# Background projections by 512 columns and half of the tokens, in place of 256 columns and all tokens, in a two-layer encoder on one Trainium2 core

## The chip, the core and the metric

The kernel runs on one core of one Trainium2 chip. The metric is the device time of one execution in microseconds. The core's engines are TensorE (PE in the profile; PEld is its weight load), VectorE (DVE), ScalarE (ACT), GpSimd (POOL) and SyncE (SP, which here issues the weight loads). Each runs its own instructions in the order in which they are written and waits for the others by semaphores.

## What is computed

Two encoder layers over 768 tokens (a prompt of 512 and a sample of 256) with 1024 channels. One combined input projection feeds a gated linear attention branch (GLA) and a grouped-query attention branch; each is gated by a SiLU and projected, and the two are merged by sigmoid gates.

```python
def layer(x, norm_g, w_in, ...):
    h = rmsnorm(x, norm_g)
    proj = h @ w_in
    qa, ka, va, gfl, gbl, za, qb, kb, vb, zb, ma, mb = jnp.split(proj, split_points(), axis=-1)
    ya = gla_branch(qa, ka, va, gfl, gbl, za, w_gate_f, b_gate_f, w_gate_b, b_gate_b,
                    gla_norm_g, w_branch_a)
    yb = attn_branch(qb, kb, vb, zb, q_norm_g, k_norm_g, w_branch_b)
    merged = jax.nn.sigmoid(ma) * ya + jax.nn.sigmoid(mb) * yb
    return x + merged @ w_out
```

In `gla_branch` the output of the linear attention is normalised per head of 256 channels, multiplied by `silu(za)` (1024 gate columns) and projected. In `attn_branch` the queries and keys are normalised per head and get rotary positions before the attention.

## The kernel before

**Products in three passes.** Everything is float32. Each operand of a large product is split into a high part (fp32r) and the rest, so a product takes three matmul passes (high by high, high by low, low by high). For a weight block SP loads `w_raw`, ACT copies it to `w_hi` (`split` on ACT, L915), POOL subtracts to make `w_lo` (`split` on POOL, L1336). The weights lie in a ring of four slots (`RING`). The ACT split number i writes the slot of block i + 3 and waits (`w_used`) until TensorE has used block i - 1; SP loads the next block into a slot once its `w_lo` is made.

**Background.** Only part of the projection is made in a stage of its own. The other columns (`qb` to `mb`, and `za`) are made as *background*: TensorE puts their passes between the small, dependent products of the later stages. A background block is one of the 8 row blocks (`KT`) of the weights by 256 columns (`BGW`), used for all six tiles of 128 tokens (`NT`), which is 6 tiles x 3 passes of 256 columns. Eight blocks finish a group of 256 columns by 768 tokens, summed in three PSUM banks (5, 6, 7; in the rotary stage alternately 2, 3, 4). ACT then copies the three banks to the staging tile `stg` (L930, `copy_sums`) and stores it to a DRAM tensor `proj` (`store`). TensorE may write a bank again when `bg_free` says that ACT has copied it.

**Stages of a layer, and the order in them.** The order is written out by hand in each engine's program.

- GLA start: ACT and VectorE compute the gates of the first head while TensorE does 8 background blocks.
- GLA heads: four heads, each of ten levels (`gla_levels`); in each level TensorE does small products, VectorE collects and scales, ACT merges, and TensorE fills in 6 to 11 background tiles (`GLA_DONE`). At level 5 ACT computes the next head's gates (L995) and then stores a finished group. 16 blocks per head.
- Rotary stage: TensorE does only background here, 5 groups = 40 blocks: one group of `zb` and the four groups of `za`. VectorE does 18 rotary pieces (`rope`, L1709, L1713, L1715), whose second factor comes from POOL (`rope_swapped`, L1382, two buffers), the normalisation of the four GLA heads (`value_norms`, L1692) and, for each `za` group, the multiplication by the SiLU that ACT left in `stg` (`gate_columns`, L1700). `sil_ready` tells VectorE that `stg` is filled, `sil_used` tells ACT that it may be overwritten. POOL does splits and rotary pieces in one queue.
- Attention: four groups of 20 softmax steps each, with 16 background blocks per group; `ATT_TILES` says how many background tiles TensorE does in each step.
- Branch and output projections: 512-column products that the change leaves alone.

A stage ends with `phase_end`: ACT, VectorE and POOL wait for all; TensorE goes on with background of the next stage where that is allowed.

Of the kernel before, what the change touches and what calls it, by code (L numbers as in the profile page):

```python
# [33 lines left out]
F32 = mybir.dt.float32  # L34
# [41 lines left out]
J_Q, J_K, J_V, J_ZB, J_MA, J_MB, NBG = 0, 4, 5, 6, 10, 14, 18  # L76
BG_BLOCKS = 2 * KT
BG_TILES = BG_BLOCKS * NT

ROPE_GROUPS = 5  # L80
# [14 lines left out]
def start_steps(block, first, done, blocks):  # L95

    return {i: -1 if i * NT < first else next((n for n, d in enumerate(done) if i * NT < d), len(done))
            for i in range(block, block + blocks)}
# [3 lines left out]
GLA_FIRST, ATT_FIRST = KT * NT, 20  # L102
# [3 lines left out]
GLA_DONE = spread(GLA_FIRST, GLA_STEPS, (1, GLA_FIRST + 4), (5, GLA_FIRST + KT * NT), (9, GLA_TURN - 6), (GLA_STEPS, GLA_TURN))  # L106
GATE_STEP = 3
ATT_TAIL = 12
ATT_TILES = (3, 3, 3, 3, 2, 2, 3, 3, 4, 2, 3, 4, 4, 4, 3, 4, 4, 3, 4, 3)
ATT_DONE = [ATT_FIRST + sum(ATT_TILES[:n + 1]) for n in range(GROUP * UNITS)]  # L110
assert ATT_DONE[-1] == BG_TILES - ATT_TAIL and KT * NT in ATT_DONE
ATT_PIECE = 9
assert [ATT_DONE[ATT_PIECE + i] for i in (-1, 0)] == [KT * NT - 2, KT * NT]
PAIR_END = (1, 3, 4)
ATT_START = start_steps(0, ATT_FIRST, ATT_DONE, BG_BLOCKS)
GLA_START = start_steps(GLA_FIRST // NT, GLA_FIRST, GLA_DONE, BG_BLOCKS)
# [218 lines left out]
def trunk(nc, x_prompt, x_sample, norm_g, w_in, w_gate_f, b_gate_f, w_gate_b, b_gate_b, gla_norm_g,  # L335
# [37 lines left out]
    stg = sb("stg", [P, NT, BGW], R_G)  # L373
    proj = nc.dram_tensor("proj", [P, NBG, NT, BGW], F32, kind="Internal")
# [102 lines left out]
    with nc.Block() as block:  # L477

        @block.sync
        def _(sp):  # L480
# [26 lines left out]
            for layer in range(DEPTH):  # L507
# [5 lines left out]
                load_group(w_in, layer, C_QB, BGW)  # L513
                with at.repeat(GH, "gla background") as h:
                    for i in range(2):
                        load_group(w_in, layer, h * (2 * BGW) + C_QB + BGW + i * BGW, BGW)
                load_group(w_in, layer, C_ZB + 3 * BGW, BGW)
                with at.repeat(4, "rope background") as i:
                    load_group(w_in, layer, i * BGW + C_ZA, BGW)
                with at.repeat(KVH, "attention background") as g:  # L520
                    for i in range(2):
                        load_group(w_in, layer, g * (2 * BGW) + C_MA + i * BGW, BGW)
# [12 lines left out]
        def _(pe):  # L535
# [28 lines left out]
            def background(start, stop, bank0=BG_BANK, spare=0, ends=False):  # L564


                for u in range(start, stop):
                    i, t = divmod(u, NT)
                    k = i % KT
                    if t == 0:  # L570
# [4 lines left out]
                    out = ps[:, bank0 * HALF + t * BGW:bank0 * HALF + (t + 1) * BGW]  # L575
# [1337 lines left out]
```

## Time and profile before

| | us |
|---|---|
| median of 3 runs (2059.82 to 2060.16) | 2059.89 |
| the profiled execution's own time | 2061.01 |
| its span, first to last instruction | 2059.1 |
| TensorE matmul busy in the span | 1967.9 (96%) |
| VectorE, ACT, POOL busy | 987.4, 919.0, 736.1 |

The span is one execution as the hardware profiler saw it. The time that an execution reports is a little longer than the span. Matmuls are pipelined, so the busy time of single matmuls overlaps; the distance from start to start is what a pass costs. PEclk is the granted share of TensorE's full clock.

### The profile page before, as it was taken

What the parts mean: (1) busy time and instruction counts of PE and PEld (TensorE: products, weight loads), DVE (VectorE), ACT (ScalarE), POOL (GpSimd) and SP (SyncE); (2) the same over time, 40 slices, a digit from 0 to 9 for tenths busy, and PEclk for the clock granted to TensorE, in tenths of its full rate; (3) what the DMA queues carried; (4) which work ended last, traced back from release to release, by engine and by line L of the source; (5) the groups of instructions that cost most, each with busy time, mean ns of one, the idle gap of its engine ahead of it and who ended that gap; (6) DMA issues with size and microseconds to landing.
All of it is one profiled execution on the core that took longest, in us unless ns stands there. A gap on an engine that the chain in (4) does not pass through costs nothing.

```text
span 2059.1 us, 37278 instructions
## 1 busy us (share of the span) xinstructions
PE 1967.9 (96%) x13184; PEld 1817.1 (88%) x13184; DVE 987.4 (48%) x1397; ACT 919.0 (45%) x1816; POOL 736.1 (36%) x744
## 2 busy tenths in 40 slices
PE   5998999999999998999999989999999999989997
PEld 4988999999999997887799889999999999978786
DVE  4112555569755654324241045557686555633224
ACT  4213445533556665422441145545336656643233
POOL 3433222248432331333553332222682332323244
PEclk9999999999999999999999999999999999999999
DMA  4321222432121114331432121225221111152323
GB/s 146 93 59 42 73 60 66 139 102 65 37 65 46 56 46 145 111 117 62 126 98 77 51 57 62 66 69 158 81 58 47 46 61 53 54 175 71 118 87 138
DMA packets 122923, 168.92 MB, mean 82 GB/s; under 512 B 15696, under 2 KB 89296, under 8 KB 122832
## 3 DMA queue, kind: packets, MB, share of 16 engines
q1 hardware_dynamic: 82656, 107.52, 18.3%
q10 hardware_dynamic: 40176, 60.18, 8.5%
q8 instruction: 59, 0.97, 0.2%
q14 instruction: 32, 0.26, 0.0%
HBM read 136.19 MB, written 31.46 MB: 81 GB/s over the span
## 4 chain that ended last, share of the span: by engine, by line
PE 86%; DVE 5%; ACT 4%; issue 2%; ACTq 1%; DMA 1%; POOL 0%; DVEq 0%
PE ps L578 11%; PE ps L579 11%; PE ps L580 11%; PE ps L540 10%; PE ps L542 10%; PE ps L541 10%; PE ps L708 5%; PE ps L723 3%; PE ps L764 3%; PE ps L661 2%; PE ps L779 2%; PE ps L780 2%; PE ps L729 2%; PE ps L752 1%; PE ps L753 1%
## 5 line engine op out<-in xcount | busy, mean ns | idle before, releaser
L1336 POOL TENSOR_TENSOR w_lo<-w_raw,w_hi 128x256 fp32r<-128x256 f32 (+1 forms) x560 | 586.8, 1055 | 1254.6 <-ACT w_hi L915 1252.8
L578 PE MATMUL ps<-w_hi,act_hi 128*128 128x256 f32 x2112 | 611.6, 290 | 13.8 <-POOL w_lo L1336 8.6
L580 PE MATMUL ps<-w_hi,act_lo 128*128 128x256 f32 x2112 | 598.5, 283 | 0.0
L579 PE MATMUL ps<-w_lo,act_hi 128*128 128x256 f32 x2112 | 598.4, 283 | 0.0
L915 ACT ACTIVATE w_hi<-w_raw 128x256 fp32r<-128x256 f32 (+1 forms) x560 | 275.7, 501 | 515.1 <-PE ps L542 300.7
L578 PEld LDWEIGHTS ps<-w_hi,act_hi 128*128 128x128 f32 x2112 | 405.0, 192 | 19.9 <-POOL w_lo L1336 9.4
L579 PEld LDWEIGHTS ps<-w_lo,act_hi 128*128 128x128 f32 x2112 | 405.4, 192 | 2.7
L580 PEld LDWEIGHTS ps<-w_hi,act_lo 128*128 128x128 f32 x2112 | 405.2, 192 | 0.0
L540 PE MATMUL ps<-w_hi,o_hi 128*128 128x512 f32 x384 | 157.6, 410 | 9.3 <-DVE o_lo L1507 6.9
L542 PE MATMUL ps<-w_hi,o_lo 128*128 128x512 f32 x384 | 152.1, 396 | 0.0
L541 PE MATMUL ps<-w_lo,o_hi 128*128 128x512 f32 x384 | 151.7, 395 | 0.0
L1739 DVE TENSOR_REDUCE st<-ps 128x1 f32<-128x512 f32 (+1 forms) x160 | 109.4, 688 | 85.9 <-PE ps L753 85.9
L1094 ACT ACTIVATE pr<-ps,st 128x512 f32<-128x512 f32 (+1 forms) x192 | 117.2, 612 | 49.9 <-DVE st L1739 47.6
L1025 ACT ACTIVATE scaled<-scaled 128x768 f32<-128x768 f32 x64 | 53.3, 833 | 162.6 <-DVE scaled L1599 161.7
L1745 DVE TENSOR_TENSOR pt_lo<-ps,pt_hi 128x512 fp32r<-128x512 f32 x128 | 88.0, 688 | 45.2 <-ACT pt_hi L1104 42.9
L1104 ACT ACTIVATE pt_hi<-ps 128x512 fp32r<-128x512 f32 x128 | 76.6, 599 | 67.0 <-PE ps L780 52.4
L1615 DVE COPY_PREDICATED amat<-mask,ps 128x768 f32<-128x768 uint8 x56 | 58.0, 1036 | 99.0 <-issue 79.2
L708 PE MATMUL ps<-scaled 128*128 128x128 f32 x768 | 102.3, 283 | 0.0
L764 PE MATMUL ps<-ident,pr 128*128 128x128 f32 x640 | 96.3, 273 | 3.6 <-ACTq L1096 3.6
L540 PEld LDWEIGHTS ps<-w_hi,o_hi 128*128 128x128 f32 x384 | 73.5, 191 | 28.9 <-DVE o_lo L1507 7.5
L708 PEld LDWEIGHTS ps<-scaled 128*128 128x128 f32 x768 | 96.9, 192 | 0.3
L542 PEld LDWEIGHTS ps<-w_hi,o_lo 128*128 128x128 f32 x384 | 73.2, 191 | 16.1
(174 smaller groups left out, 3574.2 us busy)
## 6 DMA issues: line engine op xcount, KB each, us to landing
w_raw<-in_w_in SPq DMA_DIRECT2D x352, 128.0 KB, 2.1
proj<-stg ACTq DMA_DIRECT2D x36, 768.0 KB, 3.5
w_raw<-in_w_in SPq DMA_DIRECT2D x80, 256.0 KB, 2.7
w_raw<-in_w_out SPq DMA_DIRECT2D x64, 256.0 KB, 2.7
w_raw<-in_w_branch_a SPq DMA_DIRECT2D x32, 256.0 KB, 2.7
w_raw<-in_w_branch_b SPq DMA_DIRECT2D x32, 256.0 KB, 2.7
q<-proj ACTq DMA_DIRECT2D x8, 768.0 KB, 4.9
zb<-proj ACTq DMA_DIRECT2D x8, 768.0 KB, 9.7
```

Of the source, the lines that this page charges most:

```text
L540: mm(out, s_hi, m_hi, start=first, stop=False)
L541: mm(out, s_hi, m_lo, start=False, stop=False)
L542: return mm(out, s_lo, m_hi, start=False, stop=last)
L578: mm(out, act_hi[:, k, tok], w_hi[:, k % RING, 0:BGW], start=(k == 0 and t % 2 == 0), stop=False, skip_group_check=True)
L579: mm(out, act_hi[:, k, tok], w_lo[:, k % RING, 0:BGW], start=False, stop=False, skip_group_check=True)
L580: last = mm(out, act_lo[:, k, tok], w_hi[:, k % RING, 0:BGW], start=False, stop=(k == KT - 1), skip_group_check=True)
L708: last = mm(ps[:, j * P:(j + 1) * P], lhs, rhs, start=True, stop=True)
L764: last = nc.tensor.transpose(bank(pt_bank(n))[:, place * P:(place + 1) * P], pr[:, n % 2, j * P:(j + 1) * P], ident[:])
L915: A(w_hi[:, slot, 0:width], w_raw[:, slot, 0:width], ACT.Copy).then_inc(s.w_hi_done, 1)
L1094: last = A(pr[:, n % 2, i * w:(i + 1) * w], ps[:, n % 2 * HALF + i * w:n % 2 * HALF + (i + 1) * w], ACT.Exp, bias=nmax(n, i), accum_out=de ...
L1336: G.tensor_tensor(w_lo[:, slot, 0:width], w_raw[:, slot, 0:width], w_hi[:, slot, 0:width].bitcast(F32), ALU.subtract).then_inc(s.w_lo_done, 1)
L1739: V.tensor_reduce(out, view_ps(n % 2 * HALF, (HALF // k, k), (1, HALF // k)), AX.X, ALU.max, negate=True).then_inc(s.neg_max, 1)
```

## The change

A background block becomes 512 columns wide and serves three token tiles (`NH`), half of the tokens: 3 tiles x 3 passes of 512 columns. A pair of such groups (`pair`, half 0 and half 1) makes 512 columns for all tokens, so each weight block is loaded and split twice, once per half, in the GLA and attention stages. The number of blocks there stays (8, 16 per head, 16 per attention group); the tables of tiles per step are about halved. A tile fills a PSUM bank of its own.

In the rotary stage the 40 blocks become 24: the 1024 `za` columns are made as two groups of 512 columns for **all six** token tiles (`gate_columns` on TensorE, banks 5, 6, 7, 0, 1, 2 and then 3, 4, 5, 6, 7, 0), 8 blocks each of 6 tiles x 3 passes of 512 columns; then one half group of 8 blocks in banks 1, 2, 3. ACT still stages three tiles at a time in `stg`, so a six-tile group is handed to VectorE in two halves. VectorE's multiplications (now `gate_values`) and the `value_norms` stand at other rotary pieces, and the last one comes before the stage's end. POOL's rotary pieces are spread by `rope_block`. In the attention group the reciprocal of the sums (`sums_inverse(0)`) stands one step earlier.

```diff
+GATE_BANKS = (5, 6, 7, 0, 1, 2), (3, 4, 5, 6, 7, 0), 1
+ROPE_BLOCKS = 3 * KT
+def rope_block(n):
+    at = n * 5 * KT // (3 * NT)
+    return at // 2 if at < 4 * KT else at - 2 * KT
...
-ATT_TILES = (3, 3, 3, 3, 2, 2, 3, 3, 4, 2, 3, 4, 4, 4, 3, 4, 4, 3, 4, 3)
+ATT_TILES = (2, 1, 1, 2, 1, 1, 2, 1, 2, 1, 1, 2, 2, 2, 2, 1, 2, 2, 2, 2)
...
-    stg = sb("stg", [P, NT, BGW], R_G)
+    stg = sb("stg", [P, NH, HALF], R_G)
...
-                    if k == 0 and t % 2 == 0:
-                        pe.wait_ge(s.bg_free, at.peek("bg_free", 1 - 3 * spare))
+                    if k == 0:
+                        pe.wait_ge(s.bg_free, at.peek("bg_free", NH + 1 - back))
                         at.skip("bg_free", 1)
-                    mm(out, act_hi[:, k, tok], w_hi[:, k % RING, 0:BGW], ...)
-                    mm(out, act_hi[:, k, tok], w_lo[:, k % RING, 0:BGW], ...)
-                    last = mm(out, act_lo[:, k, tok], w_hi[:, k % RING, 0:BGW], ...)
+                    t = i // KT % 2 * NH + n
+                    last = three_passes(bank(bank0 + n), act_hi[:, k, t * P:(t + 1) * P], act_lo[:, k, t * P:(t + 1) * P],
+                                        w_hi[:, k % RING, :], w_lo[:, k % RING, :], k == 0, k == KT - 1)
...
+            def gate_columns(banks, behind):
+                def tile(k, t):
+                    if k == 0:
+                        if t == behind:
+                            pe.wait_ge(s.o_read, at.peek("o_read", 2))
+                            pe.sem_inc(s.passed, 1)
+                        pe.wait_ge(s.bg_free, at.peek("bg_free", NH + 1 - (NH if behind and t < NH else 8)))
+                        at.skip("bg_free", 1)
...
+                gate_columns(GATE_BANKS[0], NT - 1)
+                gate_columns(GATE_BANKS[1], None)
+                background(BG_HALF, 2 * BG_HALF, GATE_BANKS[2], 8)
...
-                for i in range(ROPE_GROUPS * KT):
-                    split(i % KT, BGW)
+                for i in range(ROPE_BLOCKS):
+                    split(i % KT)
                     if i == 0:
                         rsqrt_seed(NT * GH)
+                    if i in (KT - 1, KT, 2 * KT - 1, 2 * KT):
+                        pair, half = divmod(i - KT + 1, KT)
+                        if i == KT - 1:
+                            all_stored()
+                        else:
+                            act.wait_ge(s.sil_used, at("sil_used"))
+                        for n in range(NH):
...
+                            A(stg[:, n, :], bank(GATE_BANKS[pair][half * NH + n]), ACT.Silu).then_inc(s.bg_free, 1)
+                        act.wait_ge(s.bg_free, at("bg_free", NH))
+                        act.sem_inc(s.sil_ready, 1)
+                act.wait_ge(s.sil_used, at("sil_used"))
+                store(P_GATE, 1, GATE_BANKS[2])
...
-                    if n in (3, 7, 11):
-                        value_norms(n // 4)
-                    if n in (6, 10, 14):
-                        gate_columns(n // 4 - 1)
-                value_norms(3)
+                    if n in (2, 4, 10, 12):
+                        value_norms((2, 4, 10, 12).index(n))
+                    if n in (7, 8):
+                        gate_values(n - 7)
+                    if n == 14:
+                        gate_values(2)
+                        gate_values(3)
```

**VectorE in the rotary stage.** This is VectorE's queue before, from the norm behind rotary piece 3 to the first multiplication by a SiLU (`rot` are the rotary buffers, `va` the GLA values, `stg` ACT's staging tile).

```order
L1692 SCALAR_TENSOR_TENSOR va<-va,st,gv_row 128x256 x5
L1709 TENSOR_TENSOR rot_103<-q,cs 128x512
L1713 TENSOR_TENSOR rot_103<-rot_103,rot_104 128x512 [waits rot2_ready,dve_chain]
L1715 TENSOR_TENSOR q<-rot_103,st_qk 128x512 [waits dve_chain]
L1709 TENSOR_TENSOR rot_103<-kv,cs 128x256 [waits rot2_free]
L1713 TENSOR_TENSOR rot_103<-rot_103,rot_104 128x256 [waits rot2_ready,dve_chain]
L1715 TENSOR_TENSOR kv<-rot_103,st_qk 128x256 [waits dve_chain]
L1709 TENSOR_TENSOR rot_103<-q,cs 128x512 [waits rot2_free]
L1713 TENSOR_TENSOR rot_103<-rot_103,rot_104 128x512 [waits rot2_ready,dve_chain]
L1715 TENSOR_TENSOR q<-rot_103,st_qk 128x512 [waits dve_chain]
L1700 TENSOR_TENSOR va<-va,stg 128x6x256 [waits va_normed,sil_ready,rot2_free]
```

And now, from the second of the two norms that stand before it (piece 4) to the second multiplication.

```order
L1725 SCALAR_TENSOR_TENSOR va<-va,st,gv_row 128x256 x5
L1744 TENSOR_TENSOR rot_103<-kv,cs 128x256
L1748 TENSOR_TENSOR rot_103<-rot_103,rot_104 128x256 [waits rot2_ready,dve_chain]
L1750 TENSOR_TENSOR kv<-rot_103,st_qk 128x256 [waits dve_chain]
...
L1750 TENSOR_TENSOR q<-rot_103,st_qk 128x512 [waits dve_chain]
L1735 TENSOR_TENSOR va<-va,stg 128x3x512 [waits va_normed,sil_ready,rot2_free]
L1744 TENSOR_TENSOR rot_103<-kv,cs 128x256
L1748 TENSOR_TENSOR rot_103<-rot_103,rot_104 128x256 [waits rot2_ready,dve_chain]
L1750 TENSOR_TENSOR kv<-rot_103,st_qk 128x256 [waits dve_chain]
L1735 TENSOR_TENSOR va<-va,stg 128x3x512 [waits sil_ready,rot2_free]
```

The first multiplication has moved from behind piece 6 and one norm to behind piece 7 and two norms.

**ACT in the rotary stage.** Before, where a SiLU group ends: splits, the three copies of the finished group, and the next splits (`w_hi` are the split weights).

```order
L915 ACTIVATE w_hi<-w_raw 128x256 [waits w_used,w_slot2]
L930 ACT_TABLE_LOAD [waits stored]
L930 ACTIVATE stg<-ps 128x512 [waits w_used]
L930 ACTIVATE stg<-ps 128x512 x2
L915 ACTIVATE w_hi<-w_raw 128x256 [waits bg_free,w_used,w_slot3]
L915 ACTIVATE w_hi<-w_raw 128x256 [waits w_used,w_slot0]
```

And now.

```order
L944 ACTIVATE w_hi<-w_raw 128x512 [waits w_used,w_slot2]
L1260 ACT_TABLE_LOAD [waits bg_done]
L1260 ACTIVATE stg<-ps 128x512 [waits stored]
L1260 ACTIVATE stg<-ps 128x512 [waits bg_done] x2
L944 ACTIVATE w_hi<-w_raw 128x512 [waits bg_free,w_used,w_slot3]
L1260 ACTIVATE stg<-ps 128x512 [waits bg_done,sil_used]
L1260 ACTIVATE stg<-ps 128x512 [waits bg_done]
L1260 ACTIVATE stg<-ps 128x512 [waits w_used]
L944 ACTIVATE w_hi<-w_raw 128x512 [waits bg_free,w_used,w_slot0]
L944 ACTIVATE w_hi<-w_raw 128x512 [waits w_used,w_slot1]
```

Three copies stand at a group's end and one split later three more, which wait for `sil_used`, with all later splits behind them.

**POOL in the rotary stage.** Before, two or three `w_lo` of 256 columns stand between two rotary pieces (`rot_104` is POOL's factor).

```order
L1336 TENSOR_TENSOR w_lo<-w_raw,w_hi 128x256 [waits w_hi_done] x3
L1382 TENSOR_TENSOR rot_104<-q,cs 128x16x16 [waits rot2_free]
L1382 TENSOR_TENSOR rot_104<-q,cs 128x16x16
L1336 TENSOR_TENSOR w_lo<-w_raw,w_hi 128x256 [waits w_hi_done] x2
L1382 TENSOR_TENSOR rot_104<-q,cs 128x16x16 [waits rot2_free]
```

Now, from the end of piece 8 over the two splits behind it to piece 9 and one more split.

```order
L1415 TENSOR_TENSOR rot_104<-kv,cs 128x8x16
L1369 TENSOR_TENSOR w_lo<-w_raw,w_hi 128x512 [waits w_hi_done] x2
L1415 TENSOR_TENSOR rot_104<-q,cs 128x16x16 [waits rot2_free]
L1415 TENSOR_TENSOR rot_104<-q,cs 128x16x16
L1369 TENSOR_TENSOR w_lo<-w_raw,w_hi 128x512 [waits w_hi_done]
```

Each piece of POOL stands behind the split of its block, so behind TensorE's progress by blocks of twice the length.

## Rows read from the trace of the kernel before

**Rows 1.** The page's chain that ended last, shares of the span by engine.

```profile
PE 86%; DVE 5%; ACT 4%; issue 2%; ACTq 1%; DMA 1%; POOL 0%; DVEq 0%
```

**Rows 2.** Busy time in the stages of layer 0, from GLA start to attention.

```profile
core 0: us, PE busy (x) PEld busy (x) DVE busy (x) ACT busy (x) POOL busy (x), PEclk, DMA share, GB/s
178.30:202.70 24.40, 20.09 (x149) 19.60 (x150) 6.63 (x6) 14.69 (x17) 7.67 (x8) 0.93 0.15 39
202.70:438.50 235.80, 233.91 (x1789) 227.56 (x1788) 133.28 (x167) 114.75 (x197) 56.18 (x73) 1.00 0.29 89
438.50:527.00 88.50, 87.76 (x729) 87.59 (x730) 75.11 (x87) 29.56 (x71) 70.53 (x76) 1.00 0.26 71
527.00:810.00 283.00, 275.17 (x2177) 263.11 (x2175) 164.37 (x278) 176.14 (x418) 88.21 (x104) 1.00 0.17 53
```

**Rows 3.** Timeline, TensorE, passes of 256 columns: start, length in us.

```profile
600.00 0.28 PE L578 MATMUL ps<-w_hi,act_hi 128*128 128x256 f32 x1
...
600.36 0.28 PE L578 MATMUL ps<-w_hi,act_hi 128*128 128x256 f32 x1
```

**Rows 4.** Timeline, TensorE, passes of 512 columns.

```profile
149.79 0.39 PE L542 MATMUL ps<-w_hi,act_lo 128*128 128x512 f32 x1
...
150.47 0.39 PE L542 MATMUL ps<-w_hi,act_lo 128*128 128x512 f32 x1
```

**Rows 5.** Groups of POOL by shape: busy us, mean ns of one.

```profile
L1336 POOL TENSOR_TENSOR w_lo<-w_raw,w_hi 128x512 fp32r<-128x512 f32 x232 | 315.5, 1365 | 551.2 <-ACT w_hi L915 551.1
L1336 POOL TENSOR_TENSOR w_lo<-w_raw,w_hi 128x256 fp32r<-128x256 f32 x328 | 271.3, 836 | 703.4 <-ACT w_hi L915 701.7 <-issue 1.0
```

**Rows 6.** Groups of ACT by shape.

```profile
L915 ACT ACTIVATE w_hi<-w_raw 128x512 fp32r<-128x512 f32 x232 | 144.6, 629 | 357.6 <-PE ps L542 300.7 <-PEq L561 29.4 <-PEq L631 8.0
L915 ACT ACTIVATE w_hi<-w_raw 128x256 fp32r<-128x256 f32 x328 | 131.1, 411 | 157.5 <-PE ps L580 140.2 <-ACT stg L930 8.4 <-issue 4.3
```

**Rows 7.** Timeline, TensorE: rotary start, first key transpose behind the stage.

```profile
438.55 0.36 PE L578 MATMUL ps<-w_hi,act_hi 128*128 128x256 f32 x1 [0.29 <-issue]
...
530.27 0.82 PE L729 MATMUL ps<-ident,k_st 128*128 128x128 f32 x6
```

**Rows 8.** Timeline, VectorE, rotary stage; piece 7 ends before 480.04.

```profile
442.78 0.68 DVE L1709 TENSOR_TENSOR rot<-q,cs 128x512 f32<-128x512 f32 x1
...
460.18 4.97 DVE L1692 SCALAR_TENSOR_TENSOR va<-va,st,gv_row 128x256 f32<-128x256 f32 x6
...
475.08 1.76 DVE L1700 TENSOR_TENSOR va<-va,stg 128x1536 f32<-128x1536 f32 x1 [1.55 <-ACTq L1230]
...
480.04 4.48 DVE L1692 SCALAR_TENSOR_TENSOR va<-va,st,gv_row 128x256 f32<-128x256 f32 x6
```

**Rows 9.** Timeline, VectorE, end of the rotary stage.

```profile
524.67 2.46 DVE L1692 SCALAR_TENSOR_TENSOR va<-va,st,gv_row 128x256 f32<-128x256 f32 x6
527.55 1.76 DVE L1700 TENSOR_TENSOR va<-va,stg 128x1536 f32<-128x1536 f32 x1 [0.41 <-ACTq L462]
```

**Rows 10.** Timeline, ACT, first key copy of the attention.

```profile
529.00 0.85 ACT L1137 ACTIVATE k_st<-kv 128x768 fp32r x1
```

**Rows 11.** Groups of POOL in the rotary stage, by shape.

```profile
L1382 POOL TENSOR_TENSOR rot<-q,cs 128x256 f32<-128x256 f32 x24 | 24.4, 1038 | 0.0
```

**Rows 12.** Timeline, POOL, GLA start.

```profile
192.43 4.17 POOL L1336 TENSOR_TENSOR w_lo<-w_raw,w_hi 128x256 fp32r<-128x256 f32 x4 [3.85 <-ACT w_hi L915]
```

**Rows 13.** Timeline, TensorE, GLA start: the idle time before it.

```profile
194.59 0.48 PE L578 MATMUL ps<-w_hi,act_hi 128*128 128x256 f32 x1 [3.53 <-POOL w_lo L1336]
```

**Rows 14.** Timeline, ACT, level 5 of a GLA head.

```profile
285.73 1.67 ACT L995 ACTIVATE gate<-ps,bg_fix 128x768 f32<-128x768 f32 x2
...
287.60 1.57 ACT L930 ACTIVATE stg<-ps 128x512 f32<-128x512 f32 x3
```

**Rows 15.** Timeline, TensorE, level 5 of the last GLA head.

```profile
406.39 0.36 PE L578 MATMUL ps<-w_hi,act_hi 128*128 128x256 f32 x1 [1.57 <-ACT stg L930]
```

**Rows 16.** Waits of TensorE in the attention: us in total, times, longest.

```profile
PE ps L779 <- DVE q L1764: 1.7, 4, 0.4
```

More of the change, by code:

```diff
@@ L95, in start_steps @@
 def start_steps(block, first, done, blocks):
-    return {i: -1 if i * NT < first else next((n for n, d in enumerate(done) if i * NT < d), len(done))
+    return {i: -1 if i * NH < first else next((n for n, d in enumerate(done) if i * NH < d), len(done))
             for i in range(block, block + blocks)}
-GLA_FIRST, ATT_FIRST = KT * NT, 20
+GLA_FIRST, ATT_FIRST = BG_HALF, 10
 GLA_STEPS = len(LEVELS) + 1
@@ L574, in background @@
                         at.skip("bg_free", 1)
-                    out = ps[:, bank0 * HALF + t * BGW:bank0 * HALF + (t + 1) * BGW]
-                    tok = slice(t * P, (t + 1) * P)
-                    mm(out, act_hi[:, k, tok], w_hi[:, k % RING, 0:BGW], start=(k == 0 and t % 2 == 0), stop=False, skip_group_check=True)
-                    mm(out, act_hi[:, k, tok], w_lo[:, k % RING, 0:BGW], start=False, stop=False, skip_group_check=True)
-                    last = mm(out, act_lo[:, k, tok], w_hi[:, k % RING, 0:BGW], start=False, stop=(k == KT - 1), skip_group_check=True)
@@ L584, in background @@
                         last.then_inc(s.bg_done, 1)
+            def gate_columns(banks, behind):
[6 more added lines that the diff above has]
+                        at.skip("bg_free", 1)
+                    last = three_passes(bank(banks[t]), act_hi[:, k, t * P:(t + 1) * P], act_lo[:, k, t * P:(t + 1) * P],
+                                        w_hi[:, k % RING, :], w_lo[:, k % RING, :], k == 0, k == KT - 1)
+                    if k == KT - 1 and t < NT - 1:
+                        last.then_inc(s.bg_done, 1)
+                    return last
+                for k in range(KT):
+                    pe.wait_ge(s.w_lo_done, at("w_lo_done"))
+                    late = behind is not None and k < 2
+                    for t in range(NT - late):
+                        last = tile(k, t)
+                    if not late:
+                        last.then_inc(s.w_used, 1)
+                    elif k == 1:
+                        for early in range(2):
+                            tile(early, NT - 1).then_inc(s.w_used, 1)
@@ L787, in turn_out @@
                     at.skip("o_drained", 1)
[L789 removed]
+                background(0, 6)
                 for part in range(2):
@@ L1422, in attention_group @@
                         h += 1
-                    split(i, BGW if i + SKEW < BG_BLOCKS else HALF)
+                    split(i)
                 assert h == GROUP
@@ L1441, in _ @@
                 phase_ends()
-                for i in range(GLA_FIRST // NT):
-                    split(i, BGW)
+                for i in range(KT):
+                    split(i)
                 with at.repeat(GH - 1, "gla head") as h:
```

123 lines of the change are left out of this document (55 added, 68 removed).

## The prediction

> **What bounds the kernel now.** The chain of work that ended last comes first: 86% of it is TensorE [rows 1]. The stages then say how closely TensorE is packed: in the GLA heads it is busy for 233.9 of 235.8 us, in the rotary stage for 87.8 of 88.5, in the attention for 275.2 of 283.0 [rows 2]. So in those stages a shorter TensorE program shortens the kernel as long as nobody becomes later than it. In the rotary stage the reader should also see VectorE at 75.1 and POOL at 70.5 of 88.5 us [rows 2]: the next bound is near. The second layer repeats the first; I work out one layer and double it.
>
> **What the change gives TensorE.** Full-clock passes of 256 columns follow each other at 120 ns (three in 0.36 us, [rows 3]), passes of 512 columns at 227 ns (three in 0.68, [rows 4]). Two of the old are 240 ns, one new is 227: 13.3 ns less. A layer has 9 + 5 + 8 = 22 groups of 8 blocks x 18 passes = 3168 old passes, 1584 new ones: 1584 x 13.3 = 21.1 us, 42.2 for both layers. By stage: GLA start 1.0, GLA heads 7.7, rotary 4.8, attention 7.7. The price is in splits. A 512-column w_lo takes POOL 1.37 us and w_hi takes ACT 0.63, against 0.84 and 0.41 for 256 [rows 5, 6]. Over a block of 9 x 227 ns = 2.04 us this fits. The weight loads double in bytes; they run blocks ahead and I price them at nothing, since no load stands among TensorE's waits.
>
> The Trainium skill, page "TensorE: Matmul & The Clock Gate", section "Back-to-back issue gap", speaks against the change: start to start is columns / 2.4 GHz plus 2.5 ns. By it a merged pair saves only 2.5 ns, an estimated 8 us for both layers. The trace does not agree: over the streaming it shows 13 ns at both widths.
>
> **GLA start: +0.6.** TensorE waits 3.53 us for a w_lo here and then runs at half clock (granted clock 0.93 over 24.4 us, so 3.4 us at half, a loss of 1.7) [rows 2, 13]. ACT's gate functions stand ahead of the split. Each split on this path gets 0.22 longer on ACT and some 0.5 on POOL, or more: four w_lo of 256 took 4.17 there [rows 12], against 0.84 mean. I take +0.9 for the late w_lo, less 0.3 for the three blocks behind it: +0.6. The block behind it hides the rest. The wait was 3.5 and becomes 3.8, so the clock's loss stays.
>
> POOL's share of that wait bears on a rule of the Trainium skill, page "SBUF — State Buffer", section "Who interferes with whom": a VectorE operation with two SBUF inputs and a GpSimd one exclude each other for a whole instruction. By it a w_lo of 512 can hold VectorE for 1.3 us where one of 256 held it for 0.7, but half as often; the sum stays.
>
> **GLA heads: -4.3.** All 64 blocks save 7.7. At level 5 the gain is lost. ACT does gate magnitudes (285.73, 1.67 us), one split and then the first copy of the finished group, started at 287.60 and done 0.6 later [rows 14]; TensorE may not start the next group before. The background tiles ahead of this point shrink from 11 x 0.36 = 3.96 to 5 x 0.68 = 3.4, the ACT path grows by 0.2: per head 0.55 + 0.3 = 0.85 is waited instead of gained. In the last head, which already waits 1.57 there [rows 15], 0.6. Together 3 x 0.85 + 0.6 = 3.2, rounded with 0.2 for steps that now have 3.4 us of cover in place of 3.6 to 4.0: 7.7 - 3.4 = 4.3.
>
> **Attention: -7.5.** 4 x 16 blocks save 7.7. Where a group starts, the key transposes and the first scores wait for VectorE, not for background: there 0.2 a group is lost, 0.8 in all. Steps cut from 3 tiles (1.08 us) to 1 (0.68) stay above the chain, since TensorE waits little here, and one of its waits, 0.4 us a group before the value products [rows 16], is eased by the reciprocal that now stands a step earlier: 4 x 0.4 = 1.6 gained at most; I take 0.6, between that and nothing. So -7.7 + 0.8 - 0.6 = -7.5.
>
> **Rotary stage: +8.2, the term that decides.** TensorE starts at 438.55 [rows 7]. A six-tile block is 18 x 227 ns = 4.09 us. Group 0 ends at 471.3. Group 1 uses banks 3, 4, 5, 6, 7, 0; its last tile of its first block needs bank 0, which tile 3 of group 0 filled. TensorE gets there at 438.55 + 8 x 4.09 + 5 x 0.68 = 474.7. But ACT copies tile 3 only after `sil_used`, behind VectorE's first multiplication, and that now stands behind pieces 0 to 7 **and two norms**. In the trace VectorE ended piece 7 at 480.0, with one norm and the old multiplication (1.76 plus 1.55 waiting) done [rows 8]. Take these 3.3 out, put the second norm in (4.48) and the multiplication behind (1.76): 480.0 - 3.3 + 4.5 + 1.8 = 483.0, less 0.6 since POOL is a little less crowded: 482.4. A copy (0.6) later TensorE goes on: 483.1, after 8.4 us of waiting and with 1.7 lost to half clock as at the GLA start. Blocks 8 and 9 end at 483.1 + 4.77 + 1.7 = 489.6.
>
> The hold travels. POOL's piece 9 stands behind the split that needs block 9 used: 489.6 + 0.63 (ACT) + 1.3 (POOL) + 2 x 0.8 (piece; 1.04 each when crowded, [rows 11]) = 493.1, and VectorE, which wants it near 486.5, waits 6 us. From there its work up to the third multiplication is 5 pieces of about 2.8, two norms of 4.4, one multiplication of 1.8 and 2 us of waits: 493.1 + 26.6 = about 519.5. ACT stands before that with split 17 and all later ones behind it: three copies (1.6) and the split, w_lo at 522. POOL then has 7 splits of 1.3 and three pieces (1.7, 1.7, 1.3) = 13.8: stage end near 535.7. Before, it was when VectorE's last norm ended, 527.13 [rows 9], and the first key transpose on TensorE came 3.1 later, at 530.27 [rows 7, 10]. Now it comes at 538.8: 8.5 later; the 0.3 of background that is not hidden any more is given back. I take +8.2. TensorE's own gain of 4.8 is inside this number. Bounds from rows: below, the stage can't end before VectorE's work is done. That starts at 442.8 [rows 8]; 75.1 us of it [rows 2], 1.8 for the multiplication that moved in, 2.0 for the handover between the third and the fourth, 3 for the wait at the first piece: 524.7, or -2.4. Above, each later split on POOL as long as when crowded (1.4 to 2.1 a piece of w_lo) and a second half-clock stretch: +13.
>
> **Sum.** 0.6 - 4.3 + 8.2 - 7.5 = -3.0 a layer, -6.0 for both. The profiled execution took 2061.0, so 2055.0 for it; the median of the runs is 1.1 lower: **2054**.
>
> **Rivals.** A change of 0.2%, 4.1 us, is what a measurement of this kernel can tell.
> - *The rotary hold is light.* If VectorE speeds up whenever POOL stands idle (its norms took 2.46 in place of 4.97 with POOL quiet, [rows 8, 9]), the multiplication comes earlier, the cascade through piece 9 shrinks, and the stage ends within 0 to +6. Time 2038 to 2050. For it: those two rows. Against: before piece 7 POOL has eight pieces and nine splits to do. Chance 0.2.
> - *The rotary hold is heavier, and the kernel slower.* The third multiplication's hold stops split 17 and everything behind it. If VectorE comes there later than 519.5, each us moves the stage end one for one, and TensorE's second idle stretch halves its clock again (1.7). From +10.3 a layer the time is unchanged, from +13.2 it is slower by 0.2%. Time 2059 to 2068. For it: VectorE is the fullest engine after TensorE, and has 6 us of waits that I estimate. Chance 0.2.
> - *A wide pass costs more in the background than alone.* 227 ns is from a stage of nothing else. At 232 the 1152 passes of GLA heads and attention a layer cost 5.8 more: 2054 + 11.5 = 2065. Against: the 256-column pass is 120 ns amid the attention's small products [rows 3]. By the skill's rule for the gap the gain outside the rotary stage would fall by 10.8 x 1152 = 12.4 us a layer, an estimate of 2079. Chance 0.08, the skill's rule within it 0.02.
>
> **How the numbers follow.** Forecast (rotary +6 to +10.3): 0.52, range 2050 to 2058. Faster: the light hold (0.2) and most of the forecast (to +9.2, 0.40) = 0.6. Same: the rest of the forecast (0.12) and half of the heavy hold (0.12) = 0.24. Slower: 0.08 + 0.08 = 0.16. The range leaves out the far ends of the light and the heavy hold: 2042 to 2065.
>
> **What the profile after would show.** Passes at 227 ns. In the rotary stage a wait of TensorE of some 8 us, ended by ACT's copy, near 475; a wait of VectorE for POOL near 487; ACT waiting for VectorE's third multiplication; first key transpose near 538. In the GLA heads a wait of about 1 us a head for the copy at level 5. Attention group 68.4 us in place of 70.3. The prediction is wrong if TensorE runs through the rotary stage (then it is far too high), or if the steps of the attention, cut to one tile, now end in waits for ACT (then too low).

## The result: slower by 1.4%, and the profile after

| | before | after |
|---|---|---|
| median, us | 2060.02 (2059.82 to 2060.34, 4 runs) | 2088.96 (2088.49 to 2090.86, 4 runs) |
| ratio | | 1.0142, 95% interval 1.0124 to 1.0160 |
| span of the profiled execution | 2059.1 | 2086.7 |
| TensorE busy, mean granted clock | 1967.9, 0.992 | 1955.1, 0.984 |
| POOL, VectorE busy | 736.1, 987.4 | 859.6, 1020.1 |

TensorE's program did get shorter and the kernel got longer: 28.9 us slower where 6 us faster was forecast. The stages say where. A stage is measured from its first TensorE instruction to that of the next one (GLA start: first gate product; heads: first level product; rotary: first background pass behind the last head; attention: first key transpose; its end: first product of the branch).

| stage, us a layer | before, layers 0, 1 | after, layers 0, 1 | change forecast | change measured |
|---|---|---|---|---|
| GLA start | 24.4, 24.4 | 25.2, 25.2 | +0.6 | +0.8 |
| GLA heads | 235.9, 235.9 | 238.4, 238.4 | -4.3 | +2.5 |
| rotary | 91.7, 91.7 | 104.1, 104.2 | +8.2 | +12.4 |
| attention | 287.5, 287.3 | 286.6, 286.7 | -7.5 | -0.8 |
| sum | | | -3.0 | +14.9 |

Twice the last sum is 29.8; the untouched stages give some 2 back, which makes the 27.6 of the spans.

Busy time by stage of layer 0 of the changed kernel, with the columns of [rows 2] (windows chosen from its own stage starts; the third ends with VectorE's last rotary piece):

```profile
core 0: us, PE busy (x) PEld busy (x) DVE busy (x) ACT busy (x) POOL busy (x), PEclk, DMA share, GB/s
176.90:202.10 25.20, 20.84 (x77) 16.12 (x78) 7.22 (x6) 16.40 (x17) 11.38 (x8) 0.86 0.27 73
202.10:440.40 238.30, 230.86 (x1213) 197.68 (x1211) 144.67 (x167) 127.41 (x197) 92.60 (x74) 0.99 0.41 123
440.40:541.90 101.50, 87.53 (x373) 70.75 (x374) 79.88 (x88) 28.24 (x55) 66.72 (x60) 0.97 0.23 63
544.50:831.10 286.60, 273.45 (x1606) 227.56 (x1606) 167.21 (x282) 185.73 (x421) 113.24 (x103) 0.99 0.29 87
```

Read the heads first, against the second stage of [rows 2]. VectorE has the same 167 instructions and is busy for 144.7 us in place of 133.3: its own work did not change, each piece of it takes longer. The engine that did change is POOL, 92.6 in place of 56.2. The groups of POOL in the heads, before and then after:

```profile
L1336 POOL TENSOR_TENSOR w_lo<-w_raw,w_hi 128x256 fp32r<-128x256 f32 x64 | 48.8, 776 | 168.2 <-ACT w_hi L915 167.4 <-issue 0.5
```

```profile
L1369 POOL TENSOR_TENSOR w_lo<-w_raw,w_hi 128x512 fp32r<-128x512 f32 x65 | 86.3, 1345 | 134.8 <-ACT w_hi L944 134.3 <-issue 0.5
```

As many blocks, each twice as wide (the 65th lies at the window's edge): a weight block is now split once for each half of the tokens. The 37.5 us more on POOL are the price that the prediction set against TensorE's block time alone. The timeline shows them landing on VectorE. Level products of the second head, changed kernel; VectorE, POOL, TensorE, in this order:

```profile
272.81 2.04 DVE L1634 TENSOR_TENSOR scaled<-scaled,totals 128x768 f32<-128x768 f32 x1
```

```profile
270.76 3.27 POOL L1369 TENSOR_TENSOR w_lo<-w_raw,w_hi 128x512 fp32r<-128x512 f32 x2 [0.24 <-issue]
```

```profile
275.00 1.24 PE L742 MATMUL ps<-scaled 128*128 128x128 f32 x9 [0.83 <-DVE scaled L1634]
```

Two `w_lo` end at 274.03. The multiplication beside them takes 2.04 us, ends 0.8 behind them, and TensorE waits 0.83 for it. At the same place before the change it took 0.95, since two `w_lo` of 256 took 1.44 and were over:

```profile
273.57 0.95 DVE L1601 TENSOR_TENSOR scaled<-scaled,totals 128x768 f32<-128x768 f32 x1
```

```profile
271.26 1.44 POOL L1336 TENSOR_TENSOR w_lo<-w_raw,w_hi 128x256 fp32r<-128x256 f32 x2 [0.24 <-issue]
```

The last head shows it once more: multiplications of the rotary tables take 0.35 us each up to the first row below; the two behind it, beside POOL's `w_lo`, take 1.4 each (second row is the first of them). The value products behind them wait 1.23 (third fence).

```profile
426.02 0.35 DVE L1709 TENSOR_TENSOR cs<-cs_raw,g_qk 128x192 f32<-128x192 f32 x1
426.29 1.43 DVE L1706 TENSOR_TENSOR cs<-cs_raw,g_qk 128x192 f32<-128x192 f32 x1
```

```profile
426.01 2.85 POOL L1369 TENSOR_TENSOR w_lo<-w_raw,w_hi 128x512 fp32r<-128x512 f32 x2 [1.88 <-ACT w_hi L944]
```

```profile
431.28 0.70 PE L757 MATMUL ps<-va,amat 128*128 128x256 f32 x2 [1.23 <-DVEq L1674]
```

In the rotary stage the forecast waits came, and the stage was 4.2 us longer still than forecast. TensorE, ACT, VectorE:

```profile
485.75 0.80 PE L550 MATMUL ps<-w_hi,act_hi 128*128 128x512 f32 x1 [8.99 <-ACT stg L1260]
```

```profile
522.93 1.58 ACT L1260 ACTIVATE stg<-ps 128x512 f32<-128x512 f32 x3 [5.45 <-DVE va L1735]
```

```profile
483.31 1.76 DVE L1735 TENSOR_TENSOR va<-va,stg 128x1536 f32<-128x1536 f32 x1
...
495.87 0.69 DVE L1748 TENSOR_TENSOR rot<-rot,rot 128x512 f32<-128x512 f32 x1 [5.60 <-POOL rot L1415]
```

The forecast was 8.4 us of waiting, here 8.99, behind the first multiplication and ACT's copy; then VectorE waits 5.6 for piece 9 (forecast 6), and ACT stands 5.45 before the last copies of a SiLU group, until VectorE's third multiplication is done.

### The profile page after: what moved, and what is told of

It is laid out like the page before. It is cut to its first block and busy times, and to the rows that moved or that the text cites. A ratio compares the mean times of both kernels' runs of the same rounds, so it can differ in the third digit from the quotient of the medians.

```text
span 2086.7 us, 30548 instructions
## 1 busy us (share of the span) xinstructions
PE 1955.1 (94%) x10016; PEld 1642.5 (79%) x10016; DVE 1020.1 (49%) x1397; ACT 962.5 (46%) x1784; POOL 859.6 (41%) x712
## 5 line engine op out<-in xcount | busy, mean ns | idle before, releaser
L1369 POOL TENSOR_TENSOR w_lo<-w_raw,w_hi 128x512 fp32r<-128x512 f32 x528 | 715.6, 1363 | 1154.7 <-ACT w_hi L944 1153.5
L550 PE MATMUL ps<-w_hi,act_hi 128*128 128x512 f32 x1248 | 507.3, 407 | 48.3 <-ACT stg L1260 18.0
L944 ACT ACTIVATE w_hi<-w_raw 128x512 fp32r<-128x512 f32 x528 | 322.5, 625 | 488.5 <-PE ps L552 410.3
L552 PE MATMUL ps<-w_hi,act_lo 128*128 128x512 f32 x1248 | 492.5, 395 | 0.0
L551 PE MATMUL ps<-w_lo,act_hi 128*128 128x512 f32 x1248 | 492.2, 394 | 0.0
L550 PEld LDWEIGHTS ps<-w_hi,act_hi 128*128 128x128 f32 x1248 | 237.8, 191 | 100.6 <-POOL w_lo L1369 22.0
L552 PEld LDWEIGHTS ps<-w_hi,act_lo 128*128 128x128 f32 x1248 | 236.9, 190 | 52.2
L551 PEld LDWEIGHTS ps<-w_lo,act_hi 128*128 128x128 f32 x1248 | 238.2, 191 | 41.9
L742 PEld LDWEIGHTS ps<-scaled 128*128 128x128 f32 x768 | 98.2, 191 | 13.4 <-issue 4.8
L798 PEld LDWEIGHTS ps<-ident,pr 128*128 128x128 f32 x640 | 78.4, 140 | 23.0 <-issue 2.0
```

The costliest lines, as they stand in the source:

```text
L550: mm(out, s_hi, m_hi, start=first, stop=False)
L551: mm(out, s_hi, m_lo, start=False, stop=False)
L552: return mm(out, s_lo, m_hi, start=False, stop=last)
L742: last = mm(ps[:, j * P:(j + 1) * P], lhs, rhs, start=True, stop=True)
L798: last = nc.tensor.transpose(bank(pt_bank(n))[:, place * P:(place + 1) * P], pr[:, n % 2, j * P:(j + 1) * P], ident[:])
L944: A(w_hi[:, slot, 0:width], w_raw[:, slot, 0:width], ACT.Copy).then_inc(s.w_hi_done, 1)
```

## Experiments

All are compared with the changed kernel (2088.96) unless said otherwise. A stage whose program an experiment leaves alone still differs from run to run: in the changed kernel and its variants the heads took 237.8 to 239.5 us, the rotary stage 104.1 to 105.4, the attention 286.2 to 288.5. Stage differences of about 1 us are no finding.

First, what the rotary hold costs (the hold is TensorE's wait for a bank that ACT empties only behind VectorE's multiplication). A second staging tile takes the wait for VectorE away:

```diff
+    stg2 = sb("stg2", [P, NH, HALF], R_O + 7 * ROW)
...
-                        else:
+                        elif i > KT:
                             act.wait_ge(s.sil_used, at("sil_used"))
...
-                            A(stg[:, n, :], bank(GATE_BANKS[pair][half * NH + n]), ACT.Silu)
+                            A((stg2 if half else stg)[:, n, :], bank(GATE_BANKS[pair][half * NH + n]), ACT.Silu)
```

> The changed kernel with a second staging tile in the rotary stage: the gate values of tiles 3 to 5 are staged in it, so that ACT does not wait for VectorE's first (and third) multiplication; everything else as in the changed kernel. Theory A (the rotary stage is long because of the hold at bank 0 and what follows from it): TensorE's 9.0 us wait near 477 goes, with the 3.4 us at half clock behind it; ACT's wait of 5.5 us before the last copies goes too; the stage (first gate block to first key transpose, 104.1 us a layer) gets some 10 us shorter, 92 to 96, and the kernel 16 to 24 us faster than the changed one: 2065 to 2073. Theory B (VectorE and POOL are the bound of that stage, since each two-input operation of one stops the other): TensorE's wait goes as well, but the stage ends only 2 to 5 us earlier, 99 to 102: 2079 to 2085.

Measured 2077.55 us (2075.7 to 2079.35), 11.4 faster; ratio to before 1.0084 (1.0067 to 1.0101). The stage is 96.8 us in both layers. The wait near 477 is gone, and the stage is 7.3 us shorter of the 12.4. That lies between the two theories: 5.1 us a layer remain over before. TensorE has new waits in them, 3.12 us at 519.7 and 1.78 at 527.5, both for POOL's `w_lo`, with 3.4 us at half clock behind the first. The attention took 288.0 and 288.5, 1.4 and 1.8 more than in the changed kernel, with half clock at its start. Stage of layer 0 in this run, columns as above:

```profile
440.60:535.00 94.40, 88.75 (x378) 71.62 (x378) 84.09 (x88) 28.32 (x55) 74.20 (x60) 0.98 0.26 72
```

VectorE is busy for 84.1 of 94.4 us, though its work is one multiplication (1.8) more than the 75.1 of [rows 2]. The rest is stretching. The norms and the four gate multiplications of this run:

```profile
L1727 DVE SCALAR_TENSOR_TENSOR va<-va,st,gv_row 128x256 f32<-128x256 f32 x24 | 21.2, 948 | 0.1
...
L1737 DVE TENSOR_TENSOR va<-va,stg 128x1536 f32<-128x1536 f32 x4 | 10.9, 2747 | 0.1
```

2.75 us for a multiplication that takes 1.76 with POOL quiet, and 5.3 for a norm of six operations that takes 2.46 so [rows 9]. Before the change the means of this stage were 1.86 and 4.3, so some of this was there already; the two differences, 3.5 and 4.0 us in all, make the stretching.

The other way to shorten the hold is VectorE's order:

```diff
-                    if n in (7, 8):
-                        gate_values(n - 7)
+                    if n in (4, 6):
+                        gate_values((4, 6).index(n))
```

> The changed kernel with VectorE's first two gate multiplications behind rotary pieces 4 and 6 in place of 7 and 8; nothing else moves. Theory A (the hold is VectorE's order): the first multiplication ends near 477.4 in place of 485.0, TensorE's wait shrinks from 9.0 to about 2 us, piece 9 is no longer late, and the stage is 5 to 8 us shorter: 2073 to 2079. Theory B (VectorE and POOL bound the stage as a whole): the wait shrinks likewise, the stage by 0 to 3 us: 2083 to 2089.

Measured 2080.23 us (2079.47 to 2081.03); TensorE's wait at bank 0 is 1.45 us, the stage 99.6, 4.5 shorter. Again between the theories, because the hold moved: TensorE now waits 7.12 us later on, behind the third multiplication, for which ACT stands 9.96 us before its copies and the splits behind them.

```profile
524.65 0.80 PE L550 MATMUL ps<-w_hi,act_hi 128*128 128x512 f32 x1 [7.12 <-POOL w_lo L1369]
```

Next, is it POOL's splits that hold VectorE, and does the length of one matter or their sum?

```diff
-                G.tensor_tensor(w_lo[:, slot, 0:width], w_raw[:, slot, 0:width], ...
+                for c in range(0, width, width // parts):
+                    cols = slice(c, c + width // parts)
+                    last = G.tensor_tensor(w_lo[:, slot, cols], w_raw[:, slot, cols], ...
...
-                    split(i)
+                    split(i, parts=2)
```

> The changed kernel with each background w_lo on POOL (GLA heads, rotary, attention) made as two operations of 256 columns in place of one of 512, the same values. Theory A (while POOL runs a w_lo, VectorE's two-input operations stand still, so the longer w_lo is what costs the GLA heads 1 us at level 3 and stretches the rotary tail): the multiplication of VectorE at level 3 falls from 2.0 to about 1.4 us, the heads lose 0.5 to 0.9 us a head, the rotary tail 1 us, and POOL's extra 0.3 us a block is hidden: 2078 to 2084 in all. Theory B (the heads wait because steps have 5 tiles of cover and the chain is longer than that, whatever POOL does): nothing gained, POOL's longer splits cost a little: 2088 to 2093.

Measured 2094.96 us (2093.13 to 2096.36), 6 slower. The multiplication of theory A fell as it said, and the time did not:

```profile
273.73 1.50 DVE L1637 TENSOR_TENSOR scaled<-scaled,totals 128x768 f32<-128x768 f32 x1
```

The heads took 239.8 a layer, 1.5 more, since other multiplications at other levels now took 1.45 to 1.50 in place of 0.95. Cutting the hold into pieces spreads it; it takes nothing away. The pieces also cost POOL more in sum (104.0 us of `w_lo` in the heads in place of 85.0), so this run does not tell length from sum by itself. Theory A was right on the mechanism and wrong on the remedy.

The next run takes most of POOL's work away, in the same three stages:

```diff
+                for cols in [slice(0, 64 if parts == 2 else width)]:
+                    last = G.tensor_tensor(w_lo[:, slot, cols], w_raw[:, slot, cols], ...
```

> The changed kernel with each background w_lo on POOL (GLA heads, rotary, attention) cut to its first 64 columns; the other columns keep what lay in the slot, so that part of the second product is left out. It shows what POOL's splits cost in each stage. Theory A (they hold VectorE): GLA heads 238.4 falls by at least 3 us a layer, to 233 to 235.5; the rotary stage by 3 to 6 us even with the hold left in; the attention (286.6) by 1 to 3: 2062 to 2076. Theory B (their length matters little, order and cover do): heads and attention within 1 us of the changed kernel, only the rotary stage shorter by up to 3: 2080 to 2088.

Measured 2048.79 us (2048.38 to 2053.14), 40 faster than the changed kernel and, with that part left out, 0.5% faster than before (ratio 0.9954, 0.9937 to 0.9970). Heads 234.0 and 236.4, rotary 87.6 and 87.5, attention 286.4 and 286.1. In size theory A was too modest but for the attention. POOL's splits cost the heads 4.4 us (1.9 in layer 1, where TensorE waits 3.84 us at the last head's level 5 and then runs at half clock) and the rotary stage 16.5: even the wait at bank 0 shrinks from 8.99 to 0.42. VectorE is busy for 131.8 us in the heads and 57.5 in the rotary stage, in place of 144.7 and 79.9. In the rotary stage this run does not part two effects, VectorE's stretching and POOL's own queue, whose `w_lo` TensorE also waited for with two staging tiles. The attention does not care (0.2 and 0.6), against theory A. The opposite test gives the narrow kernel the wide kernel's POOL work:

```diff
-                            split(i, BGW)
+                            split(i, HALF)
...
-                    split(i, BGW if i + SKEW < BG_BLOCKS else HALF)
+                    split(i, HALF)
```

> The kernel before the change, in which POOL alone makes each background w_lo of the GLA heads and of the attention 512 columns wide, as the changed kernel does (the second 256 columns are made from what lies in the slot and are not used); TensorE, ACT, the loads and all tables are as before. Theory A (POOL's longer work, 1.36 in place of 0.84 us a block, holds VectorE and so the level chain): GLA heads 235.9 rise to 237.5 to 240 a layer, attention 287.4 by 0 to 1: 2063 to 2071. Theory B (the cover of the steps does it, POOL's time is free): heads within 0.5 us: 2059 to 2061.

Measured 2064.24 us, ratio to before 1.0020 (1.0011 to 1.0030). The heads rise from 235.9 to 238.6 and 238.5; the attention by 0.1 and 0.5. POOL's wider splits alone cost the heads 2.7 us, with TensorE's passes at 256 columns, at full clock (1.00 in both layers) and with the wait at level 5 as before (1.57); the new waits are for VectorE, 0.3 us twice and 0.81 at the last value products. Theory A holds for the heads. That the sum is the time of the changed kernel is chance: there the shorter passes and other waits come in too.

The attention asks another question: steps too coarse, or a chain?

```diff
-ATT_TILES = (2, 1, 1, 2, 1, 1, 2, 1, 2, 1, 1, 2, 2, 2, 2, 1, 2, 2, 2, 2)
+ATT_PASSES = (4, 5, 4, 5, 3, 3, 4, 5, 6, 3, 4, 6, 6, 6, 5, 6, 6, 4, 6, 5)
```

> The changed kernel with the background of the GLA heads and of the attention cut into steps by passes of 512 columns (a third of a tile) in place of whole tiles, so that each step has the cover that it had before the change: in the attention 4, 5, 4, 5, 3, 3, 4, 5, 6, 3 ... passes, one tile again between the second query transposes and the first scores, in the heads 16 or 17 passes a step in place of 5 or 6 tiles. The rotary stage is untouched. Theory A (granularity: steps cut to one tile, and the group start without cover, take the gain of the attention): attention 286.6 falls to 281 to 284 a layer; the heads, whose steps differ by half a tile only, fall by 0 to 1: 2076 to 2084. Theory B (the attention is a chain through ACT and VectorE that is as long as it was, and background only fills it): attention within 1 us of the changed kernel: 2086 to 2090.

Measured 2090.24 us (2087.02 to 2091.72), no gain in the whole; attention 285.9 and 285.4, 0.7 and 1.3 shorter. Theory A's forecast fails, but the run does not show that coarse steps cost nothing. TensorE has a wait that the changed kernel hasn't, once in each of the four groups, for ACT's copy of the finished sums:

```profile
579.91 0.50 PE L586 MATMUL ps<-w_hi,act_hi 128*128 128x512 f32 x1 [0.77 <-ACT stg L961]
```

These are 3.1 us a layer. What the finer steps gain elsewhere goes into this wait and into others for ACT; an order that copies earlier was not tried. The heads were 236.6 in both layers of this run, but 238.0 and 239.3 with the same steps in the last run below, so I count nothing for them.

> The kernel before the change with the attention stage alone changed: 512 columns by three token tiles there, in steps by passes as in the run of pass steps, the reciprocal a step earlier; GLA start, heads and rotary stage stay at 256 columns by six tiles. The tensor in DRAM has the changed kernel's layout. If the attention gains by granularity (theory A) the kernel is 4 to 12 us faster than before: 2048 to 2056. If the attention is bound by its chain (theory B), it is within 2 us of before: 2057 to 2061.

Measured 2061.97 us, ratio to before 1.0010 (1.0001 to 1.0020): just above the range of theory B, and no version that beats the kernel before. Its attention took 286.4 and 285.8, 1.1 and 1.5 less than before, with the same four waits of 0.77 us in it. The heads, whose program is the old one, took 238.4 in layer 0 (235.9 before): the wait at level 5 was 2.67 us in place of 1.57, with 3.4 us at half clock behind it. That alone takes back most of the gain. What a us of TensorE is worth there can be read by leaving some out, in both kernels:

```diff
+                    if less and n == 1:
+                        mm(... act_hi ..., w_hi ...)
+                        last = mm(... act_hi ..., w_lo ...)
```

> The changed kernel, whose attention background leaves out the third pass (low by high) of the middle token tile of each block: 16 passes of 512 columns a group less, 3.7 us of TensorE a group, 14.8 a layer; that part of the computation is left out. Theory A (the attention is bound by TensorE's passes, so the wide passes should have paid): 286.6 falls by 12 to 15 a layer. Theory B (it is near the chain through exponentials, copies and VectorE, and TensorE would wait more): it falls by 8 or less.

> The kernel before, whose attention background leaves out the third pass of every third token tile: 32 passes of 256 columns a group less, 3.8 us a group, 15.4 a layer; that part of the computation is left out. Theory A (the attention before the change is bound by TensorE): 287.4 falls by 13 to 15.4 a layer. Theory B (it was close to its chain already, so that the change could gain little): it falls by 8 or less.

Measured (2081.80 and 2043.50 us for the kernels, two executions each): attention after, 279.6 and 279.6, 7 us less for 14.5 us of passes taken out (64 x 227 ns); before, 280.0 and 277.9, 7.5 and 9.4 less for 15.4. So theory B, nearly: already before the change 40 to 50% of what TensorE saves in the attention was lost again. One such wait is in the timeline of the changed kernel, at a group's start:

```profile
618.87 0.50 PE L786 MATMUL ps<-k_hh,q_hl 128*128 128x512 f32 x1 [0.52 <-DVE q_hl L1757]
```

There the two tiles between the second query transposes and the scores are gone, and TensorE waits for VectorE. In the run of pass steps they are back, and TensorE waits 0.47 and 0.48 us at the next two places instead. That speaks for a chain and not for a hole.

Last, whether VectorE's order can free the rotary stage, alone and with all other remedies:

```diff
-                    if n in (2, 4, 10, 12):
-                        value_norms((2, 4, 10, 12).index(n))
+                    if n in (2, 4, 11):
+                        value_norms((2, 4, 11).index(n))
...
-                    if n == 14:
-                        gate_values(2)
-                        gate_values(3)
+                value_norms(3)
+                gate_values(2)
+                gate_values(3)
```

> The changed kernel with the second staging tile of the run of two stages, and with VectorE's third norm behind rotary piece 11 in place of 10, the fourth norm and the third and fourth gate multiplications behind the last piece in place of pieces 12 and 14. Theory A (what is left of the rotary stage's length over before, 96.8 against 91.7 us, comes from VectorE's norms and multiplications that now run beside POOL, 5.3 and 2.7 us in place of 2.5 and 1.8): the stage falls by 2 to 5 us to 92 to 95: 2068 to 2074. Theory B (the order of VectorE's work does not matter, its sum beside POOL does): 95.5 to 98, since ACT's last copies now also stand behind VectorE's third multiplication: 2075 to 2080.

Measured 2084.18 us (2080.12 to 2086.98), stage 100.1, slower than with the second staging tile alone. The moved work did get fast:

```profile
531.69 2.46 DVE L1727 SCALAR_TENSOR_TENSOR va<-va,st,gv_row 128x256 f32<-128x256 f32 x6
534.26 3.43 DVE L1737 TENSOR_TENSOR va<-va,stg 128x1536 f32<-128x1536 f32 x2
```

But VectorE ended no earlier (94.6 us behind the stage's start, against 94.2 with the second tile alone), since the pieces ahead of it were now the ones beside POOL, and TensorE waited 8.7 us for ACT's last copies, which stand behind the third multiplication:

```profile
536.70 0.79 PE L551 MATMUL ps<-w_hi,act_hi 128*128 128x512 f32 x1 [8.71 <-ACT stg L960]
```

Its own passes behind this wait then ended the stage. That is theory B's mechanism, beyond its range: a hold in a new place.

> The run of quiet end with the background of heads and attention in steps by passes as in the run of pass steps. The gains of the stages should add: per layer heads 1.75, attention 1, beside the run of quiet end; 5 us less than that run in all. That would be 2063 to 2070 by theory A of the run of quiet end, 2070 to 2075 by theory B; in either case not below the kernel before (2060), since POOL's second split of each weight block stays.

Measured 2079.09 us (2078.3 to 2085.21), ratio to before 1.0104 (1.0087 to 1.0121). It is 5.1 below the run of quiet end, as the sum said, though that run lay higher than either theory, and the sum came out by luck: the heads gained nothing (238.0 and 239.3 against 239.5 and 237.8, forecast 1.75 a layer), the attention 1.2 and 1.3, the rotary stage 0.8 and 0.7. All remedies together leave 19 us over the kernel before.

## Why the prediction was wrong

The forecast missed by 35 us. By stage and for both layers, 13.6 of it lie in the heads, 13.4 in the attention, 8.4 in the rotary stage.

**The bound.** "So in those stages a shorter TensorE program shortens the kernel as long as nobody becomes later than it." The condition failed. TensorE was 99% busy in the heads, but the chains beside it had little to spare: 0.6 us more on each of POOL's splits was enough to make it wait.

**Passes.** Right in the rotary stage and nearly so in the heads: 227 ns at the median. In the attention most took 227 to 236, mean 231: 576 passes by 4 ns are 2.3 us a layer that the sum gave away. The formula of the Trainium skill, page "TensorE: Matmul & The Clock Gate", section "Back-to-back issue gap" (2.5 ns over columns / 2.4 GHz), does not hold here: 227 ns are 14 over the streaming. The Trainium skill gives that formula for an isolated pass, which the prediction did not say; for a stream with weight loads the same section has some 131 ns at 512 columns, and this trace does not agree with that either.

**GLA start, +0.6, measured +0.8.** Right in size, not in detail: two waits of 1.97 and 2.37 us in place of one of 3.8, each with 3.4 us at half clock behind it (granted clock 0.86, before 0.93).

**GLA heads, -4.3, measured +2.5: the first step that failed.** The step is the price of the splits, "Over a block of 9 x 227 ns = 2.04 us this fits", and with it the sentence on the rule of the Trainium skill, "the sum stays". The Trainium skill, page "SBUF — State Buffer", section "Who interferes with whom", says that a VectorE operation with two SBUF inputs contends with a GpSimd one that reads SBUF; the traces agree (2.04 beside a `w_lo`, 0.95 without). I weighed it as twice the length, half as often. It was not half as often: the heads kept 64 blocks, so POOL's splits went from 48.8 to 86.3 us, and the run that widens POOL's splits alone puts 2.7 us on the heads of the old kernel. Start to start, the passes saved their 7.5 us in the heads, and 10.0 came against them: 2.7 in waits at level 5 (0.75 in each of three heads, 2.11 in place of 1.57 in the last, forecast 3.2 in all; there the sum says that ACT's path grows by 0.2 and adds 0.3, and 0.2 would have given the 0.75), 1.7 at half clock behind the last of these, which I had not counted, 2.3 in level products that waited for VectorE (0.2 forecast), 1.4 at the last value products, and 1.9 in passes and products that each took a little longer. Of the 6.8 us by which this stage missed, the waits for VectorE are 3.5; the half clock (1.7) and the slower passes (1.9) are not shown to come from POOL.

**Attention, -7.5, measured -0.8: the second step that failed, as large as the first.** It has two parts. "Steps cut from 3 tiles (1.08 us) to 1 (0.68) stay above the chain, since TensorE waits little here" took busy time for a bound; passes left out returned half. And the 0.2 at a group's start was mis-sized (0.52 each), since I overlooked that the change removes the two tiles before the first scores. POOL is not a cause here. The eased wait at the value products came as forecast (1.7 to 1.0 us). Start to start, in layer 0, the distances behind background passes fell by 7.4 us: 5.0 in the passes themselves, 2.4 in a wait for ACT behind a group's first scores, which is gone. All other distances grew by 6.5. The largest parts are some 3 before the first scores, 1.7 between scores and the next query transposes, 1.0 before value products and 0.9 in the last transposes. So the saved time came back as waits of the small products. Which engine's work sets the length of this chain stays open. A group took 70.0 us, where 68.4 was forecast.

**Rotary, +8.2, measured +12.4.** The mechanism was right, and its sizes fell short: first multiplication forecast at 482.4, at 485.0 with a stage that began 1.9 later; wait 8.4, measured 8.99; piece 9 at 493.1, VectorE's wait for it ended at 495.87; third multiplication 519.5, measured 522.9, so 1.5 later than the shift. From there to the start of split 17's `w_lo` it is 2.5 us, as forecast. The term that was mis-sized is POOL's tail, seven splits and three pieces: 13.8, measured 16.2. Its `w_lo` took 2.08 beside the fourth multiplication and 1.37 to 1.49 behind that, where 1.3 was put. The lower bound of -2.4 was wrong in kind: it took VectorE's durations as given. Without the hold at bank 0 the stage was still 5.1 over before.

**Rivals.** The sign came from none of them. "The rotary hold is heavier" reached 2068 and had the right mechanism, for one stage; it missed that heads and attention would give nothing. (Its 2068 also lies above the sum's own upper bound: +13 in the rotary stage makes 2063.5; and a change of less than 0.2% begins at +9.2, not at +10.3.) "A wide pass costs more in the background" was true by 4 ns in the attention, 4.6 us of the 35 by which the forecast missed.

## What to carry to other kernels

When a change makes one engine's operations longer or more, ask which engine it shares a resource with, and look for its durations beside and without it, before pricing it against the bottleneck's block time. Count the total of the work that comes in, not the length of one piece: halving the pieces moved the wait, raised the total and lost time. When an experiment takes one wait away, look for the wait that takes its place before reading the gain: several of the runs here had one. And an engine that is busy for 97 to 99% is not the only bound: leave a little of its work out, and see how much of it comes back.

## What was not expected of the hardware

One and the same VectorE operation has several durations, depending on POOL: a gate multiplication 1.76 and 2.75 us, a norm of six operations 2.46 and 5.38 (in the run of early values), a table multiplication 0.35 and 1.43. POOL's `w_lo` of 512 columns likewise ranged from 1.29 to 2.08. Two `w_lo` of 256 in a row did not let VectorE through without loss (1.50 in place of 0.95).

TensorE's idle stretch of 8.99 us ended under half clock: granted 0.5 from 482.11 for 6.8 us in layer 0, so its first seven passes ran at 1.2 GHz (0.43 us from start to start in place of 0.23). In layer 1 the same wait had 10.2 us of it, but most of that fell into the wait, and again some seven passes were slow.
